# Hyena convolution: the sums of the complex products moved from GpSimd to VectorE

## The reference, cut to what matters

```python
filt_f = jnp.fft.rfft(hyena_filters(L, lp), n=2 * L, axis=0)
resp = filt_f[:, 0] + jnp.conj(filt_f[:, 1])
z = v
for o, gate in enumerate((x1, x2)):
    zf = jnp.fft.rfft(z, n=2 * L, axis=1)
    conv = jnp.fft.irfft(zf * resp[None, :, o], n=2 * L, axis=1)[:, :L]
    z = gate * (conv + z * bias[o])
```

## Time and profile before

| what | value |
|---|---|
| median of 3 runs | 4688.24 us (4680.4 to 4697.21) |
| the profiled execution: time, span | 4689.33 us, 4687.5 us |
| mean granted TensorE clock | 0.937 of full speed |
| busy over the span: PE, DVE, ACT, POOL | 88%, 52%, 22%, 25% |
| convolution stage, first product to the end of the spread | 3113.6 to 3557.6 us |
| GpSimd's sums L2144 and L2145, 40 each | 56.5 and 58.1 us busy |

### The profile page before, as it was taken

The page is one execution under the profiler, slowest core; times in us unless marked ns, Lnnn a source line. Parts: engine busy times, 40 slices in busy tenths (PEclk is TensorE's granted clock), DMA queues, the critical chain, the costliest instruction groups (busy, mean ns, idle before and its releaser), DMA issues.

```text
span 4687.5 us, 50772 instructions
## 1 busy us (share of the span) xinstructions
PE 4110.0 (88%) x21784; PEld 3429.5 (73%) x21784; DVE 2458.4 (52%) x2646; ACT 1017.6 (22%) x1384; POOL 1178.8 (25%) x586
## 2 busy tenths in 40 slices
PE   6699888778697999999959999996677799999998
PEld 3488777777475888888747777775566588888886
DVE  1466155555416444455447666579992454444453
ACT  1234122211213111111133333311111311111112
POOL 1221133333233222222231000012231422222224
PEclk8799799999798999999979999998888899999999
DMA  9511000000111111111122222232221011111111
GB/s 351 206 52 37 33 1 1 1 1 1 72 37 36 37 41 36 41 36 37 36 78 65 83 80 87 80 144 83 100 111 36 23 37 36 37 37 41 38 39 63
DMA packets 265336, 280.44 MB, mean 60 GB/s; under 512 B 9221, under 2 KB 221142, under 8 KB 261623
## 3 DMA queue, kind: packets, MB, share of 16 engines
q1 hardware_dynamic: 265112, 277.18, 17.5%
HBM read 219.48 MB, written 57.67 MB: 59 GB/s over the span
## 4 chain that ended last, share of the span: by engine, by line
PE 70%; DVE 19%; DMA 4%; issue 3%; ACT 2%; POOL 1%; SPq 1%; POOLq 0%; DVEq 0%; ACTq 0%
PE PS L590 52%; DVE piece L1470 8%; PE PS L1538 5%; DVE piece L1019 3%; DMA piece<-in_l_ada_w 2%; PE PS L990 2%; PE PS L991 2%; PE PS L986 2%; DVE piece L516 2%; PE PS L1711 1%; PE PS L702 1%; DMA piece<-hyena_tokens 1%; DVE piece L1406 1%; DVE piece L509 1%; DVE piece L1879 0%
## 5 line engine op out<-in xcount | busy, mean ns | idle before, releaser
L590 PE MATMUL PS<-piece,piece 128*128 128x512 f32 (+1 forms) x13824 | 2757.3, 361 | 150.7 <-POOL piece L534 94.5
L590 PEld LDWEIGHTS PS<-piece,piece 128*128 128x128 f32 x13824 | 2304.4, 190 | 600.7 <-issue 160.7
L573 POOL TENSOR_TENSOR piece<-piece,piece 128x1024 fp32r<-128x1024 f32 (+1 forms) x204 | 504.7, 2475 | 2417.9 <-ACT piece L567 2417.9
L1538 PE MATMUL PS<-piece,piece 128*128 128x256 f32 x1920 | 441.3, 392 | 126.1 <-DVE piece L2165 110.8
L1406 DVE SCALAR_TENSOR_TENSOR piece<-piece,piece,piece 128x1024 f32<-128x1024 f32 x352 | 534.9, 1520 | 12.6
L1538 PEld LDWEIGHTS PS<-piece,piece 128*128 128x128 f32 x1920 | 376.4, 197 | 186.1 <-DVE piece L2165 113.6
L1426 DVE SCALAR_TENSOR_TENSOR piece<-PS,piece,piece 128x1024 f32<-128x1024 f32 x224 | 187.7, 879 | 415.0 <-PE PS L590 415.0
L567 ACT ACTIVATE piece<-piece 128x1024 fp32r<-128x1024 f32 (+1 forms) x204 | 205.1, 1007 | 671.4 <-PE PS L590 634.5
L1019 DVE TENSOR_TENSOR piece<-piece,PS 128x512 f32<-128x512 f32 x288 | 185.3, 684 | 249.6 <-PE PS L991 192.3
L1403 DVE TENSOR_SCALAR piece<-piece,piece 128x1024 f32<-128x1024 f32 x44 | 35.7, 812 | 482.4 <-ACT piece L1367 482.4
L1125 POOL TENSOR_TENSOR piece<-piece,piece 128x512 f32<-128x512 f32 x120 | 159.8, 1345 | 123.9 <-PE PS L986 123.2
(11 more groups left out here) (206 smaller groups left out, 3719.1 us busy)
## 6 DMA issues: line engine op xcount, KB each, us to landing
piece<-in_l_ada_w SPq DMA_DIRECT2D x24, 2048.0 KB, 18.1
piece<-in_l_ffn_up SPq DMA_DIRECT2D x88, 512.0 KB, 3.7
piece<-in_l_w_in SPq DMA_DIRECT2D x44, 512.0 KB, 3.8
piece<-in_l_ffn_down SPq DMA_DIRECT2D x48, 384.0 KB, 3.0
piece<-filters_s SPq DMA_DIRECT2D x8, 2176.0 KB, 10.5
filters_s<-piece SPq DMA_DIRECT2D x64, 256.0 KB, 2.0
hyena_tokens<-piece SPq DMA_DIRECT2D x24, 640.0 KB, 4.0
piece<-hyena_tokens SPq DMA_DIRECT2D x12, 1280.0 KB, 5.7
```

Of the source, the lines that this page charges most:

```text
L573: eng.tensor_tensor(LO[i % 2][0][:, 0:n], RAW[i % raws][:, 0:n], HI[i % 2][1][:, 0:n], ALU.subtract)\
L590: m = eng.matmul(PS[:, bank + b, 0:n], w, x[:, a:a + n], start=first and n_ == 0, stop=last and n_ == 2)
L1538: m = eng.matmul(PS[:, bank, o * HC:(o + 1) * HC], M[i][o], rhs[i], start=i == 0, stop=i == 1)
```

## The change

The sums are issued by VectorE in `multiply`, right behind the cross product that completes a pair of leaves, with the same operands and shapes, and counted under a new semaphore name. The "re" sum waits for that cross product through VectorE's own semaphore; the "im" sum has no wait. GpSimd's loop over the stage is removed. Everything that waited for a sum still waits for the same step.

```diff
-                smC[g] = steps("po_sum_" + g, [f"{t}{a}" for a in L[::2] for t in ("re", "im")], nj)
+                smC[g] = steps("ve_sum_" + g, [f"{t}{a}" for a in L[::2] for t in ("re", "im")], nj)
...
-            @program("po")
-            def _(eng):
-                for rnd in range(nj):
-                    for g in "ps":
-                        K, T = KB2[rnd % 2][g], TB2[rnd % 2][g]
-                        for a in LEAVES[g][::2]:
-                            kr, ki, tr, ti = quarters(K, T, a)
-                            eng.wait_ge(veC[g].sem, veC[g].at(taken(g, a + 1), rnd))
-                            eng.tensor_tensor(kr, kr, ti, ALU.subtract).then_inc(*smC[g].did(f"re{a}", rnd))
-                            eng.tensor_tensor(ki, ki, tr, ALU.add).then_inc(*smC[g].did(f"im{a}", rnd))
...
                         eng.tensor_tensor(keep, both, near, ALU.mult).then_inc(*ve.did(f"near{l}", rnd))
                         eng.tensor_tensor(other, both, cross, ALU.mult).then_inc(*ve.did(f"cross{l}", rnd))
+                        if (l + n) % 2 == 0:
+                            a = l + n - 2
+                            kr, ki, tr, ti = quarters(K, T, a)
+                            eng.wait_ge(ve.sem, ve.at(f"cross{l}", rnd))
+                            eng.tensor_tensor(kr, kr, ti, ALU.subtract).then_inc(*smC[g].did(f"re{a}", rnd))
+                            eng.tensor_tensor(ki, ki, tr, ALU.add).then_inc(*smC[g].did(f"im{a}", rnd))
```

## The result

The kernel after takes 4710.39 us (median of 10 runs, 4700.68 to 4719.6), the kernel before 4688.36 us (10 runs beside them). The ratio is 1.0045, with a 95% interval of 1.0036 to 1.0054: 22 us slower, between 17 and 25. The forecast was 4708 us and slower.

A forecast was written before the change was run, and what follows sets the result against it. VectorE was taken to bound four rounds, with holes in three others. The terms 16.4 + 2.7 + 1.3 - 0.5 = 19.9 us, on the median of 4688.24, gave 4708 us, 0.42% slower, range 4698 to 4722.

The forecast's parts named there:

- The price of a sum: VectorE's ten sums a round: 1.33 us a pair including an own wait of 0.11, 6.65 us a round.
- The heads: First four tree operations of the next chunk: 3.94 us each head without GpSimd, 13.3 to 13.9 us back in all.
- Rival (a): Tree heads do not shorten because something else stretched them: 30 us slower, 4718 us; chance 0.06.
- rival (c): Not slower: GpSimd takes more from VectorE than the heads show, in the products beside it; 4688 or below; chance 0.03.
- Rounds 1, 2, 5, 6: VectorE-bound rounds: sums' 6.65 us less head and leaf-wait gains, 4.1, 4.05, 4.15 and 4.1 us longer, 16.4 in all.
- The waits for leaf 7: VectorE's wait before a round's last pair of products: gone, since VectorE comes 4.0 us later; 3.0 us over rounds 1 to 6.
- those of round 0: VectorE's waits for leaves in round 0, 4.8 of the 7.8 us: the only product waits to remain.
- Rounds 3 and 4: TensorE's burst and the gate's factor load still end last, 1.33 us later: each round 1.33 us longer, 2.7 in all.
- The low clock level: TensorE's 1.2 GHz at burst starts on the path, rounds 3, 4, 7: longest adds 1.8 us, shortest takes 2.5.
- Round 7: Only the first pair of sums lies ahead of TensorE's burst, with no tree to hide the rest: 1.3 us longer.
- The hole: VectorE's 11.1 us idle in round 7, waiting for ScalarE's last eviction: shrinks by some 5 us.
- Round 0: Sums fill the waits for leaves and tokens, and the tree's head is 1.13 us shorter: -0.5 us.

The follow-up runs named there:

- giving one pair away: After, with only the prompt group's pair of sums, first in a round, given back to GpSimd; 4698.51 us, ratio to before 1.0012.
- the deferred kernel: After, with each pair of sums issued one batch of products later, so its cross product is never the instruction just ahead; 4703.86 us, ratio to before 1.0029.
- the last-pair-on-GpSimd kernel: After, with only the sums of leaves 6 and 7 given back to GpSimd, beside the tree's head; 4713.05 us, ratio to before 1.0046.
- the second one of after: The kernel after, unchanged, run once more beside before; 4709.96 us, ratio to before 1.0035, stage 462.1 us.
- the no-sums kernel: The ten sums of every round left out on both engines, inverses waiting for the cross products; 4676.06 us, ratio to before 0.9977.

## Why the prediction was right, step by step

**The price of a sum.** Forecast 0.11 + 0.61 + 0.61 = 1.33 us a pair; 3177.19 to 3178.40 after an own wait of 0.11 is 1.32, and giving one pair away saved 1.34 a round. That VectorE's own wait costs something is told by rows and by the deferred kernel, 0.13 us a wait. The semaphore that "costs nothing extra" (the Trainium skill, "VectorE: DVE Perf Modes", "The DRAIN you can't avoid") is not what is seen here. The same section adds, and the prediction left out, that a next operation which is not held starts earlier; the 0.60 us agree with that.

**The heads.** Forecast: all 13.3 to 13.9 us come back. The grouped rows of after, the answer to the earlier trace rows, with the new sums and the large products:

```profile
L1470 DVE TENSOR_TENSOR piece<-piece 128x1024 f32<-128x1024 f32 x46 | 56.3, 1224 | 1.3
L1470 DVE TENSOR_TENSOR piece<-piece 128x512 f32<-128x512 f32 x78 | 53.9, 691 | 12.3 <-ACT piece L2130 9.9
...
L2153 DVE TENSOR_TENSOR piece<-PS,piece 128x1024 f32<-128x1024 f32 x24 | 29.2, 1218 | 0.0
...
L2159 DVE TENSOR_TENSOR piece<-piece,piece 128x512 f32<-128x512 f32 x40 | 27.7, 692 | 1.4
L2160 DVE TENSOR_TENSOR piece<-piece,piece 128x512 f32<-128x512 f32 x40 | 27.4, 684 | 0.0
```

64.6 + 59.6 became 56.3 + 53.9: 14.0 us back. Rival (a) is out. The products stayed at 1.218 us (1.215 before), so rival (c), that GpSimd costs them something, is out too. The Trainium skill, "SBUF — State Buffer", "Who interferes with whom", draws the line at the same place (two SBUF inputs against a GpSimd read) and calls the shared port pair an exclusive lock; the turns in the head of the last-pair-on-GpSimd kernel agree with it.

**Rounds 1, 2, 5, 6.** Forecast +4.1, +4.05, +4.15, +4.1; measured +4.05, +4.04, +4.06, +4.02. The waits for leaf 7 went as told; those of round 0, which were said to stay, went too.

**Rounds 3 and 4** are the step that was off. Forecast +1.33 each, since TensorE's burst and the load behind it would still end last; measured +0.23 and +0.68. Round 3 of after:

```profile
3292.12 22.92 PE L1538 MATMUL PS<-piece,piece 128*128 128x256 f32 x96 [18.67 <-DVE piece L2154]
...
3299.53 0.60 ACT L2130 ACTIVATE piece<-PS 128x512 f32<-128x512 f32 x1 [39.27 <-PE PS L1538]
...
3315.73 2.40 PE L2085 MATMUL PS<-piece,piece 128*128 128x128 f32 x20 [0.69 <-ACT piece L2130]
...
3318.16 0.32 SPq L2066 DMA_DIRECT2D piece<-hyena_tokens  x1
...
3320.21 2.88 DVE L2166 TENSOR_TENSOR piece<-PS,piece 128x1280 fp32r<-128x1280 f32 x2
...
3323.76 0.69 DVE L2174 SCALAR_TENSOR_TENSOR piece<-piece,piece 128x512 f32<-128x512 f32 x1
```

The burst did start 1.33 us later relative to the round (5.06 after the first product, 3.72 before). But from its start to the first inverse's eviction it took 7.41 us and not 8.53, and to the turn 23.6 and not 24.7. The low clock level, 1.2 GHz, which the prediction left as a term of 2 us either way, came out shorter, in round 4 too (6.94, 8.14 before). The granted clock of round 3 (the 0.50, 0.84 and 0.98), 3.5 to 5.5 and 5.5 to 7.5 us behind the burst's start before, and 3.9 to 5.9 us behind it after:

```profile
3282.00:3284.00 2.00, 2.00 (x6) 1.61 (x5) 2.00 (x2) 0.00 (x0) 2.00 (x3) 0.50 0.00 0
3284.00:3286.00 2.00, 2.00 (x9) 1.67 (x9) 0.87 (x2) 0.00 (x0) 2.00 (x3) 0.84 0.00 0
...
3296.00:3298.00 2.00, 2.00 (x10) 1.72 (x10) 1.97 (x3) 0.00 (x0) 0.00 (x0) 0.98 0.00 0
```

So the load was issued only 0.2 and 0.1 us later in the round than before, VectorE waited for nothing in these rounds, and its own way set their length. Its own way was forecast at +3.6 less holes of 3.3, and +4.0 less 3.2: +0.3 and +0.8, near the measured +0.2 and +0.7. My choice of which of the two chains is later was wrong; the margin I gave it was 1.0 and 0.5 us, less than the clock moves. Nor is the answer the same in every execution. In the second one of after, round 3 grew by 0.6 and VectorE waited 0.45 us for the load; round 4 grew by 0.7 without a wait:

```profile
DVE piece L2174 <- DMA piece<-hyena_tokens: 0.5, 1, 0.5
```

In the deferred kernel, whose bursts start 1.33 us earlier than after's, round 3 is shorter by 0.66, which is what the five own waits give, and round 4 ends with a wait for the load again. VectorE ended three of the four such rounds of after, the load one.

**Round 7.** Forecast +1.3, measured +1.25, for another reason. Its burst:

```profile
3522.47 23.79 PE L1538 MATMUL PS<-piece,piece 128*128 128x256 f32 x96 [19.49 <-DVE piece L2154]
...
3530.76 0.60 ACT L2130 ACTIVATE piece<-PS 128x512 f32<-128x512 f32 x1 [40.96 <-PE PS L1538]
...
3546.93 1.42 DVE L1470 TENSOR_TENSOR piece<-piece 128x512 f32<-128x512 f32 x2 [9.88 <-ACT piece L2130]
```

First eviction 8.29 us behind the start, 7.08 before: the longer low clock level puts 1.2 us more on the path, and the turn and split behind the last gate take 1.3 us less (granted clock 4 to 6 us behind the turn's start: 0.50 before, 1.00 after). Two things not forecast cancel, so this hit is luck. The hole shrank from 11.1 to 9.9 us, not by 5. I forgot that TensorE's later end moves its other edge, by 2.5 us, and that the wait of 1.5 us just ahead of it is filled first. The last 1.3 us were GpSimd's: in the kernel before, its last two sums of this round met the prompt group's sum (L2191, 1.03 us, 0.68 after) and gate (L2178, 1.65 us, 0.69 after).

```profile
3509.70 1.73 POOL L2145 TENSOR_TENSOR piece<-piece,piece 128x512 f32<-128x512 f32 x1
...
3510.33 1.65 DVE L2178 SCALAR_TENSOR_TENSOR piece<-piece,piece 128x512 f32<-128x512 f32 x1
```

So the heads were not all that GpSimd took; here the hole hid the rest.

**Round 0.** Forecast -0.5, measured -0.6.

**The sum.** 19.9 us forecast for the stage, 17.7 and 18.3 measured; the miss is rounds 3 and 4. The median moved by 22 and, the second time, by 18.5. That the first one lies above the stage's growth is scatter as far as the runs can tell. The forecast of 4708 us came nearer to the 4710.39 than its working deserves: the stage grew by 2.2 us less than forecast, and some 4 us were added outside it. In the no-sums kernel rounds 3 and 4 fell by 1.6 and 0.9 us where nothing was expected, the same clock term again: their first evictions came 6.9 and 7.3 us behind the burst's start, 1.6 and 0.8 sooner than before.

## What to carry to other kernels

GpSimd's elementwise work is free for VectorE only beside the right neighbours: beside products with a PSUM operand a sum cost nothing here, beside tensor_tensor steps with both operands in SBUF it cost VectorE 0.95 us, more than the 0.61 to 0.67 us that VectorE needs to do it itself. Price each piece of moved work by what runs next to it in the trace, and split at that border rather than moving all or nothing. Where two chains in a round end within a microsecond of each other and one of them starts TensorE from its low clock level, 1.2 GHz here, say that either may end last.

## What the runs showed that was not expected

- The low clock level (0.50 granted) at the head of TensorE's bursts, after 13 to 20 us without work, is not longer for a longer pause: the first eviction came 6.9 us behind the start after 18.8 us, and 8.3 us after 19.5 us in the same kernel. Between executions it moved the path of rounds 3, 4 and 7 by over 1 us either way, and with it which engine ends rounds 3 and 4.
- Where an instruction of VectorE with both inputs in SBUF and a sum of GpSimd overlap, the one that began later ends some 0.55 us (128x512 on VectorE) or 1.1 us (128x1024, or GpSimd's sum) behind the end of the other. The profile shows that wait as part of its duration.
- Code ahead of the change, the same in all kernels, took between 3109.3 and 3118.8 us. Differences between single executions below 10 us say nothing unless they are cut to the stage, where the rounds that VectorE ends repeat within 0.02 us in the kernel after.
- An instruction of VectorE that waits for the one just ahead starts 0.71 us behind it, one that does not 0.60, although both are shown with a duration of 0.68 to 0.69.
